# Two-layer trunk kernel: the first pass of each MLP as plain tiles, and two of four weight sums as adding transfers

## What is computed

```python
def squared_relu_mlp(h, w_up, w_down):
    return jnp.square(jax.nn.relu(h @ w_up)) @ w_down

    h = x
    for layer in range(DEPTH):
        hn = rmsnorm(h, mix_norm[layer])
...
        h = h + squared_relu_mlp(rmsnorm(h, mlp_norm[layer]), w_up[layer], w_down[layer])
    return rmsnorm(h, final_norm)
```

## Time and profile before

| | us |
|---|---|
| runs shown (3), median | 1362.69 (1361.07 to 1366.28) |
| profiled execution, its own time | 1364.89 |
| its span in the trace | 1363.1 |
| TensorE busy | 1274.8 |
| VectorE, ScalarE, GpSimd busy | 811.5, 633.2, 620.5 |

### The profile page before, as it was taken

The page is one execution under the profiler, slowest core; times in us unless marked ns, Lnnn a source line. Parts: engine busy times, 40 slices in busy tenths (PEclk is TensorE's granted clock), DMA queues, the critical chain, the costliest instruction groups (busy, mean ns, idle before and its releaser), DMA issues.

```text
span 1363.1 us, 20055 instructions
## 1 busy us (share of the span) xinstructions
PE 1274.8 (94%) x7837; PEld 1085.3 (80%) x7837; DVE 811.5 (60%) x1137; ACT 633.2 (46%) x1024; POOL 620.5 (46%) x681
## 2 busy tenths in 40 slices
PE   6999988879999999999999999999968999999997
PEld 5777666778888988978788778888768897888976
DVE  4537665893472743744689956476785273572753
ACT  5345665553261542634582535643535263361541
POOL 4653324827346174364455533222746517265081
...
GB/s 275 93 78 62 53 12 46 108 93 125 30 152 96 67 147 35 124 61 64 78 49 76 81 59 47 2 2 32 124 53 135 61 108 125 40 143 81 94 31 62
DMA packets 165293, 109.22 MB, mean 80 GB/s; under 512 B 4570, under 2 KB 162512, under 8 KB 165200
## 3 DMA queue, kind: packets, MB, share of 16 engines
...
q0 software_dynamic: 416, 0.07, 0.0%
...
## 4 chain that ended last, share of the span: by engine, by line
PE 65%; DVE 22%; issue 6%; ACT 6%; DMA 1%; SPq 0%; DVEq 0%; ACTq 0%
PE ps L1200 8%; PE ps L1201 8%; PE ps L1202 8%; PE ps L1080 5%; PE ps L1081 5%; PE ps L1082 5%; PE ps L1180 3%; PE ps L1182 3%; PE ps L1181 3%; DVE hid_lo L2378 3%; PE ps L1067 3%; DVE arena L2372 2%; DVE wx_lo L2339 2%; DVE relu L2372 1%; DVE w_lo L2339 1%
## 5 line engine op out<-in xcount | busy, mean ns | idle before, releaser
L953 POOL TENSOR_TENSOR w_lo<-raw_w,w_hi 128x256 fp32r<-128x256 f32 x248 | 214.4, 895 | 277.1 <-ACT w_hi L1685 277.1
L2383 DVE TENSOR_TENSOR h<-h,ps 128x512 f32<-128x512 f32 x64 | 44.0, 687 | 219.9 <-PE ps L1202 219.9
L1080 PE MATMUL ps<-hn_hi,w_hi 128*128 128x512 f32 x368 | 154.3, 419 | 0.1
L1081 PE MATMUL ps<-hn_lo,w_hi 128*128 128x512 f32 x368 | 147.2, 400 | 0.0
L1082 PE MATMUL ps<-hn_hi,w_lo 128*128 128x512 f32 x368 | 147.0, 399 | 0.0
L1022 POOL TENSOR_TENSOR w_lo<-y_mix,w_hi 128x256 fp32r<-128x256 f32 x80 | 67.2, 870 | 148.7 <-ACT w_hi L1751 148.7
L1022 POOL TENSOR_TENSOR wx_lo<-y_mix,wx_hi 128x256 fp32r<-128x256 f32 x80 | 69.0, 893 | 137.3 <-ACT wx_hi L1751 137.3
L1751 ACT ACTIVATE wx_hi<-raw_w 128x1024 fp32r<-128x1024 f32 x56 | 59.2, 1057 | 109.5 <-PE ps L1202 82.9
L1200 PE MATMUL ps<-hid_hi,w_hi 128*128 128x512 f32 x256 | 101.5, 397 | 6.6 <-DVE hid_lo L2378 6.6
L1200 PE MATMUL ps<-hid_hi,wx_hi 128*128 128x512 f32 x256 | 100.7, 393 | 7.1 <-DVE hid_lo L2378 7.1
L1751 ACT ACTIVATE w_hi<-raw_w 128x1024 fp32r<-128x1024 f32 x56 | 59.2, 1057 | 99.0 <-PE ps L1202 83.0
...
## 6 DMA issues: line engine op xcount, KB each, us to landing
raw_w<-in_w_up SPq DMA_DIRECT2D x32, 512.0 KB, 4.4
y_mix<-in_w_up SPq DMA_DIRECT2D x32, 512.0 KB, 4.4
raw_w<-in_w_down SPq DMA_DIRECT2D x32, 512.0 KB, 3.6
y_mix<-in_w_down SPq DMA_DIRECT2D x32, 512.0 KB, 4.4
raw_w<-in_o_w_in SPq DMA_DIRECT2D x27, 512.0 KB, 3.8
raw_w<-in_e_w_in SPq DMA_DIRECT2D x19, 512.0 KB, 3.8
raw_w<-in_e_w_out SPq DMA_DIRECT2D x8, 512.0 KB, 3.6
raw_w<-in_o_w_out SPq DMA_DIRECT2D x8, 512.0 KB, 3.5
```

The lines of the kernel that those rows point to most:

```text
L953: nc.gpsimd.tensor_tensor(w_lo[:, n % CUT, ks], raw_w[:, n % RING, ks], w_hi[:, n % CUT, ks].bitcast(F32), ALU.subtract).then_inc(w_cut, 1)
L1080: mm(o, a_hi, b_hi, start=(k == 0), stop=False)
L1081: mm(o, a_hi, b_lo, start=False, stop=False)
L2383: V.tensor_tensor(h[:, j, :], h[:, j, :], ps[:, D_BANK + j % 2, :], ALU.add).then_inc(added, 1)
```

## The change

**First pass of each MLP.** Its up half is 8 plain tiles (plain_up): 8 k x 3 matmuls of 512 columns into bank j % 6; the norm's matmul follows tile 0. Weights are whole columns of w_up, loaded through A0, A1, B0, B1 in turn and cut by GpSimd alone. project_out no longer makes differences: it cuts hn whole. ScalarE's and VectorE's lists for the pass are new: hidden_whole(j) makes one hidden tile, and between them stand gain_pair, part, part_high_of and part_low_of for the passes that follow, with the third difference kept in place E1 until tile 7 is done. **Down half, all passes:** tiles 0 and 1 run their first four k, then their other four; tiles 2 to 7 run k from 0 to 7. **Passes 1 to 3:** the first and third sum are transfers from GpSimd's queue, from DRAM, that add onto A and C; ScalarE copies m5 of the second half ahead of hidden(c21, 0); the quarters are combined in PSUM, and relu reads them there.

The diff, cut to its core:

```diff
+                whole_up = dram["w_up"][layer].rearrange("(k p) c -> p k c", p=P)
+                for u in range(2 * KT):
+                    if u < RING:
+                        sp.wait_ge(w_cut, PARTS * (n0 - RING + u + 1))
+                    else:
+                        unit_cut(sp, layer, 0, u - RING)
+                    load_tile(PLAIN_AT[u % 4], whole_up[:, :, u * SW:(u + 1) * SW] if u < KT else down_tile(0, u - KT))
...
+                load_up("C0", 1)
+                load_up("E0", 1)
+                unit_cut(sp, layer, 0, 2 * KT - 3)
+                load_up("A1", 1)
+                unit_cut(sp, layer, 0, 2 * KT - 2)
+                load_up("B0", 1)
+                load_up("C1", 1)
+                sp.wait_ge(part_low, 5 * (layer + 1))
+                load_up("E1", 1)
+                unit_cut(sp, layer, 0, 2 * KT - 1)
+                load_up("B1", 1)
+                for i in range(1, 4):
...
                 def sum_first(i, p):
 
-                    a_, c_ = place(layer, f"A{p}"), place(layer, f"C{p}")
                     unit_cut(pool, layer, i, U["m1", p])
-                    pool.wait_ge(u_full[f"C{p}"], 16 * (2 * (4 * layer + i) + 1))
-                    nc.gpsimd.tensor_tensor(a_, a_, c_, ALU.add).then_inc(pool_sum, 1)
+                    c0 = i * KT * SW + p * 512 + 256
+                    pool.dma_start(place(layer, f"A{p}").rearrange("p (k c) -> p k c", c=256), up[:, :, c0:c0 + 256],
+                                   accum_op=ALU.add).then_inc(first_sum[p], 16)
 
                 def sum_third(i, p):
 
-                    c_, e_ = place(layer, f"C{p}"), place(layer, f"E{p}")
-                    pool.wait_ge(u_full[f"E{p}"], 16 * (2 * (4 * layer + i) + 1))
-                    nc.gpsimd.tensor_tensor(c_, c_, e_, ALU.add).then_inc(pool_sum, 1)
-
...
+                    pool.wait_ge(u_full[f"C{p}"], 16 * LOAD_COUNT[layer, i, f"C{p}"])
+                    c0 = i * KT * SW + p * 512 + 256
+                    pool.dma_start(place(layer, f"C{p}").rearrange("p (k c) -> p k c", c=256), up_low[:, :, c0:c0 + 256],
+                                   accum_op=ALU.add).then_inc(third_sum[p], 16)
+
+                for u in range(2 * KT):
+                    low_unit(0, u)
+                for i in range(1, 4):
                     sum_first(i, 0)
-                    if i == 0:
-                        low_unit(0, 3)
                     sum_third(i, 0)
                     sum_first(i, 1)
                     sum_third(i, 1)
-                    for u in range(NUP - 2, UNITS):
+                    for u in range(NUP - 2, NUP + KT):
                         low_unit(i, u)
...
+                def plain_up(j):
+                    hi_, lo_ = (v.rearrange("p (k c) -> p k c", c=SW) for v in cut_buffers(layer, 0, j))
+                    o = ps[:, j % D_BANK, :]
+                    if j >= D_BANK:
+                        pe.wait_ge(relued, 32 * layer + j - D_BANK + 1)
+                    for k in range(KT):
+                        unit_cut(pe, layer, 0, j, k // 2 + 1)
+                        if j == 0:
+                            pe.wait_ge(normed, KT * (3 * layer + 2) + k + 1)
+                        mm(o, hi_[:, k, :], hn_hi[:, k, :], start=(k == 0), stop=False)
+                        mm(o, hi_[:, k, :], hn_lo[:, k, :], start=False, stop=False)
+                        ins = mm(o, lo_[:, k, :], hn_hi[:, k, :], start=False, stop=(k == KT - 1))
+                    ins.then_inc(u_done, 1)
...
+                def down_part(i, j, ks):
...
+                    if ks[0] == 0:
+                        n = 32 * layer + KT * i
+                        if j >= 2:
+                            pe.wait_ge(added, n + j - 1)
+                        elif n:
+                            pe.wait_ge(added, n)
+                    for k in ks:
+                        unit_cut(pe, layer, i, ups(i) + j, k // 2 + 1)
...
+                            if i == 0:
+                                pe.wait_ge(hid_ready, hid_turn(layer, 0, k))
+                            else:
+                                for c in (("c11", "c21") if k % 4 < 2 else ("c12", "c22")):
+                                    pe.wait_ge(hid_ready, hid_turn(layer, i, (c, int(k >= 4))))
+                        mm(o, hi_[:, k, :], hid_hi[:, k, :], start=(k == 0), stop=False, skip_group_check=True)
+                        mm(o, hi_[:, k, :], hid_lo[:, k, :], start=False, stop=False, skip_group_check=True)
+                        ins = mm(o, lo_[:, k, :], hid_hi[:, k, :], start=False, stop=(k == ks[-1]), skip_group_check=True)
+                    if ks[-1] != 3:
+                        ins.then_inc(u_done, 1)
...
+                    if i:
+                        first_k, other_k = DOWN_K[:4], DOWN_K[4:]
+                    else:
+                        first_k, other_k = [0, 1, 2, 3], [4, 5, 6, 7]
+                    for ks in (first_k, other_k):
+                        for j in range(2):
+                            down_part(i, j, ks)
+                    for j in range(2, KT):
+                        down_part(i, j, list(range(KT)))
...
-                    act.wait_ge(pool_sum, turn_of(POOL_SUMS, layer, i, (SUM_OF[q], p)))
+                    act.wait_ge((first_sum if q == "m5" else third_sum)[p], 16 * (pass_index(layer, i) + 1))
...
+                    drained(act, "out", layer, k)
+                    high_gained("mlp_norm", 8 * layer + k)
...
                     square(2 * layer + 1, k)
-                    if k in (2, 4, 6):
-                        part_high_of(layer, k // 2 - 1)
-                part_high_of(layer, 3)
...
+                def hidden_whole(j):
+                    t, n = relu_t[:, j % 2, :], hid_turn(layer, 0, j)
+                    act.wait_ge(relued, n)
+                    A(t, t, ACT.Square).then_inc(hid_square, 1)
+                    act.wait_ge(hid_square, n)
...
+                def gain_pair(pair):
+
+                    if pair:
+                        act.wait_ge(parted, 4 * layer + pair)
+                    for k in (2 * pair, 2 * pair + 1):
+                        A(spare[:, k % 2, :], h[:, k, :], ACT.Copy, scale=col_a("mlp_norm", 8 * layer + k)
+                          ).then_inc(gained, 1)
...
+                    act.wait_ge(parted, 4 * layer + pair + 1)
+                    A(d_hi[:, :, pair, :], d_parts[:, 1:4, :], ACT.Copy).then_inc(part_high, 1)
...
+                for u in range(KT):
+                    if u == 0:
+                        full(act, "out", layer, KT - 1)
+                        act.wait_ge(w_cut, PARTS * n0)
+                    high_unit(layer, 0, u + 3)
+                    if u == 0:
+                        norm(2 * layer + 1)
+                    hidden_whole(u)
+                    if 2 <= u <= 5:
+                        part_high_of(u - 2)
+                    if 1 <= u <= 4:
+                        gain_pair(u - 1)
...
+                        act.wait_ge(parted, 4 * layer + 4)
+                        unit_done(act, layer, 0, KT - 1)
+                        A(hn_hi[:, 0:KT:2, HT:T], place(layer, "E1").rearrange("p (k t) -> p k t", t=HT), ACT.Copy
+                          ).then_inc(part_high, 1)
+                for u in range(4):
+                    high_unit(layer, 1, u)
+                for i in range(1, 4):
...
                     high_unit(layer, i, 12)
+                    copy(i, "m5", 1)
                     hidden(i, "c21", 0)
-                    copy(i, "m5", 1)
...
-                    if k % 2:
-                        low_gained(phase, "mlp_norm", 8 * layer + k)
-                        sum_squares(2 * layer + 1, k)
-                        part(layer, k // 2)
-                    else:
...
-                        sum_squares(2 * layer + 1, k)
-                        if k:
-                            part_low_of(layer, k // 2 - 1)
-                part_low_of(layer, 3)
+                    low_gained(3 * layer + 2, "mlp_norm", 8 * layer + k)
+                    sum_squares(2 * layer + 1, k)
...
+                def hidden_whole(j):
...
+                    if j >= 2:
+                        dve.wait_ge(hid_ready, hid_turn(layer, 0, j - 2))
+                    V.scalar_tensor_tensor(out=t, in0=ps[:, j % D_BANK, :], scalar=0.0, in1=rms_t, op0=ALU.max,
+                                           op1=ALU.mult).then_inc(relued, 1)
+                    dve.wait_ge(hid_high, hid_turn(layer, 0, j))
+                    V.tensor_tensor(hid_lo[:, j, :], t, hid_hi[:, j, :].bitcast(F32), ALU.subtract
+                                    ).then_inc(hid_ready, 1)
+
+                def part(pair):
+
+                    flat = spare.rearrange("p a t -> p (a t)")
+                    dve.wait_ge(gained, KT * layer + 2 * pair + 2)
+                    if pair:
+                        dve.wait_ge(part_low, 5 * layer + pair)
+                    third = place(layer, "E1").rearrange("p (k t) -> p k t", t=HT)
```

(26 more changed lines are left out.)

266 lines of the change are left out of this document (108 added, 158 removed).

## The result

The changed kernel takes 1301.3 us (median of four runs, 1300.9 to 1305.2) against 1363.2 (1361.1 to 1366.3): the ratio is 0.955, with a 95% interval of 0.952 to 0.958. The forecast was 1311, its range began at 1304, so the gain of 61.9 us was larger than the range allowed. The profiled execution took 1301.31 us, its span is 1299.3.

What follows compares the result with a forecast made beforehand. First pass bound by VectorE and GpSimd, all others by TensorE. First passes 36.0 plus waits 15.7 gave 51.7 us off 1362.69: forecast 1311, narrow range 1306 to 1316 (0.62), wide range 1304 to 1330 (0.8).

Steps and rivals of the forecast that it cites:

- the first passes: First pass of both MLPs: from 108.75 and 108.81 us to 90.8 each, a gain of 36.0 us.
- the waits in passes 1 to 3: TensorE's waits for hid_lo (10.6 us) and for ScalarE's copy of m5 (5.1 us) vanish: 15.7 us together.
- First pass, up half: Eight tiles of 24 matmuls at 0.2335 us, 44.8, plus 0.9 for the norm's matmul: 45.7 us plus waits.
- (a) to (d): First up half: TensorE has no wait for tile 0's part 7, the norm's sum of squares, rms, or cut weights.
- (e): First pass: VectorE's chain behind rms is the tight point, 7.2 us per middle tile; 0.3 us lost per MLP.
- The two waits: Passes 1 to 3: m3's wait for m5's copy, 0.86 us, and the down half's for hid_lo, 1.0 us to spare after.
- Adding transfers: First and third weight sums in passes 1 to 3: landings of 10 us alone, 7 in a row, off the path, 0 us.
- The room of 22.9 us: Time from the first adding transfer's issue at 348.94 until m5's preparation needs it.
- The slow rival: Adding transfers above 11.5 us each (D) in a row cost 4 x (D - 11.5) per pass; D = 15 gives 1395; 0.09.
- VectorE's chain: Rival: it binds the plain first pass at 8.2 us per tile, 3.3 to 5 us more per MLP, 1318 to 1321; 0.10.
- no wait moved on: Rival: waits of passes 1 to 3 move on instead of vanishing, 7.9 us back, 1319; chance 0.10.
- the norm was not waited for: Rival: first-pass TensorE still waits at the norm, 5.7 us and some 2 us of low clock per MLP, 1327; 0.05.

Runs made afterwards that it cites:

- b_down_copy: Kernel before with only the new k order in down tiles 0 and 1 and m5's copy ahead of the last hidden quarter: 1333.5 us, ratio 0.980.
- a_again: The changed kernel unaltered, run again: 1300.5 us (1299.4 to 1301.9).
- a_sbuf: Changed kernel with only the PSUM combination undone (quarters combined in SBUF, relu reads them there): 1301.5 us (1299.5 to 1301.7).
- b_psum: Kernel before with only the quarters combined in PSUM and relu reading them there, all passes: 1380.2 us, ratio 1.013.
- a_late: Changed kernel with each pass's adding transfers issued only after unit m1 of the second half, some 19.5 us later: 1341.7 us.
- a_plain_dma: Changed kernel with accum_op left out, so the transfers overwrite instead of adding (outputs differ): 1300.6 us.

## Why the prediction was wrong by a little, point by point

The direction, the cause and the order of sizes were right; the time fell 2.7 us below the range. Three terms of the sum were too small, all in one direction: the first passes (36.0, measured 38.3), the price of the waits in passes 1 to 3 (15.7, measured 18.6), and what lies outside the MLPs (nothing, measured 6.8 in the two profiles).

- **First pass, up half: 45.7 + 0.3, measured 45.24.** No wait at part 7, the norm, rms or the cuts, as (a) to (d) said. Two sizes were off. The pace of 0.2335 us came from one tile; the tiles take 5.49 to 5.60 us, 0.229 to 0.233 per matmul, and four halves (both first passes) were overstated by 0.4 us each. The norm's matmul was sized rightly: its pair holds the tiles up by 0.86 us (0.9 reckoned). And (e): VectorE's cycle is 6.02 us, not 7.2, and nothing is late, where I took 0.3 us per MLP. Its operations mostly did not meet GpSimd's; the last low part has 4.7 us to spare, not 0.6. Together 2.3 us: first passes 38.3 instead of 36.0.
- **Passes 1 to 3: 15.7, measured 18.6.** The two waits went as described, b_down_copy shows it alone. The failed step is the price of a wait: I took the idle times of the rows. Each of the twelve cost another 0.24 us, 2.9 us in all. TensorE's rows of the kernel before around one wait:

```profile
406.01 0.40 PE L1202 MATMUL ps<-hid_hi,wx_lo 128*128 128x512 f32 x1
408.19 0.47 PE L1200 MATMUL ps<-hid_hi,wx_hi 128*128 128x512 f32 x1 [1.78 <-DVE hid_lo L2378]
408.50 0.40 PE L1201 MATMUL ps<-hid_lo,wx_hi 128*128 128x512 f32 x1
```

The starts are 2.18 us apart, where the pace is 0.23: 1.95 us are lost, not 1.78, because the idle time counts from the end of a record that the next one would have overlapped by 0.16. The start behind it comes 0.31 instead of 0.23 later, another 0.08.
- **What I had no term for: outside the MLPs, 6.8 us in the two profiles.** The sum was made against one profiled execution and took everything outside as fixed. In the profile before, the odd mixer ran at a clock of 0.96 and 356.57 us, its long length. In medians the whole gain is 61.9 (61.1 in a_again), so 4 to 5 us of it lie outside. Why the changed kernel keeps finding the short length is open, so no run here says whether this part is luck. 57.0 from the MLPs alone would have given 1306, inside the range. This and the two size errors (5.3 us) were needed to leave it, and a range with its low end only 7 us under the forecast had no place for errors that all point one way.
- **An edit I left out.** The quarters in PSUM stood in the change and got no price. In the changed kernel that was harmless (a_sbuf), but alone the edit costs 19 us (b_psum), so a slower case was missing from the rivals: a hold of VectorE by GpSimd.
- **Adding transfers: cost 0, right.** I took landings of 10 and 7 us; they are 6.4 and 8.8 in pairs, and four in a row take 3.6 to 3.9 each, below the 7 that I took and even a little below the lower bound of 4.4 for one alone. The room of 22.9 us was counted from the old issue; now they are issued at 328.4, 14 us ahead of the half, and a_late confirms the end of the room. The slow rival, D above 11.5, is far off. The Trainium skill (DMA: Bandwidth & Descriptors, Rules for kernel authors) says that an accumulating DMA reads its destination and writes it later, and gives no price. a_plain_dma agrees in so far as adding does cost time, 1.4 and 3.2 us.
- **Rivals.** VectorE's chain did not bind, no wait moved on, the norm was not waited for.
